# Both halves of the last expert pair's down products issued ahead of the products that carry tokens back, and the carrying matrix transposed between the two up products

## What is computed

```
def run_block(args):
    tok, w, e = args
    xb = x_pad[tok]
    hid = jax.nn.silu(xb @ w1[e]) * (xb @ w3[e])
    return (hid @ w2[e]) * w[:, None].astype(xb.dtype)
...
out = jnp.zeros((T + 1, D), xt.dtype).at[buf_tok].add(y.reshape(P, D))
x = x + hier_moe(rms_norm(x, norm_moe[l]), ...)
```

## Time and profile before

| what | value |
|---|---|
| median of 3 runs | 2251.21 us (2250.78 to 2253.61) |
| span of the profiled execution | 2254.1 us |
| PE busy | 2129.7 us (94%) |
| DVE busy | 743.1 us (33%) |
| ACT busy | 390.4 us (17%) |
| mean DMA rate | 235 GB/s |
| chain that ended last | PE 78%, DMA 13%, DVE 6% |

### The profile page before, as it was taken

How to read it: one execution, slowest core, us unless ns; L and a number is a source line. 1 busy time by engine, 2 the same in 40 slices (tenths; PEclk the granted TensorE clock), 3 DMA queues, 4 the chain that set the end, 5 groups by cost and what they waited for, 6 DMA issues and landing times.

```text
span 2254.1 us, 27568 instructions
## 1 busy us (share of the span) xinstructions
PE 2129.7 (94%) x11793; PEld 1133.6 (50%) x11793; DVE 743.1 (33%) x1754; ACT 390.4 (17%) x745; POOL 242.9 (11%) x250
## 2 busy tenths in 40 slices
PE   8999899999998999889999999999999999999987
PEld 4454566654443433335555567864574533333322
DVE  4125776333001011131277854422232411111104
ACT  3100132121000100011133353220022200000101
POOL 5000312000000000000001141301010000000001
PEclk9999899999999999999998999999999999999989
DMA  8113113158999999996110021124352599999998
GB/s 309 40 38 112 38 38 139 69 236 361 424 422 428 428 418 427 427 399 192 29 30 2 2 77 39 42 108 149 112 213 105 216 420 427 427 428 427 428 425 334
DMA packets 96670, 528.81 MB, mean 235 GB/s; under 512 B 10270, under 2 KB 26323, under 8 KB 69146
## 3 DMA queue, kind: packets, MB, share of 16 engines
q1 hardware_dynamic: 82304, 492.08, 53.8%
q0 software_dynamic: 8160, 17.88, 2.1%
q10 hardware_dynamic: 6074, 16.97, 2.0%
HBM read 509.04 MB, written 30.41 MB: 239 GB/s over the span
## 4 chain that ended last, share of the span: by engine, by line
PE 78%; DMA 13%; DVE 6%; ACT 1%; issue 1%; SPq 1%; ACTq 0%; DVEq 0%
PE ps L204 74%; DMA RING<-in_w_e_up 4%; DMA SC<-in_w_e_up 2%; DMA RING<-in_w 2%; DMA SC<-in_w 2%; DMA XT<-in_w 2%; DMA EX<-in_w_e_up 1%; DMA RING<-in_w_ckv 1%; PE ps L1719 1%; SPq L1633 1%; ACT SC L1876 1%; PE ps L1767 1%; PE ps L2699 0%; PE ps L3294 0%; PE ps L374 0%
## 5 line engine op out<-in xcount | busy, mean ns | idle before, releaser
L204 PE MATMUL ps<-SC 64*64 64x64 f32 (+5 forms) x5408 | 749.4, 349 | 46.7 <-ACT SC L1876 11.1
L204 PE MATMUL ps<-RING,SC 128*64 128x512 f32 (+2 forms) x1648 | 559.1, 587 | 21.6 <-ACT SC L1876 6.2
L204 PEld LDWEIGHTS ps<-SC 64*64 64x64 f32 (+2 forms) x5408 | 333.9, 146 | 345.8 <-issue 292.9
L204 PEld LDWEIGHTS ps<-RING,SC 128*64 128x64 f32 (+2 forms) x1648 | 192.9, 151 | 255.9 <-issue 244.3
L204 PE MATMUL ps<-XT,RING 128*128 128x256 f32 (+2 forms) x944 | 317.6, 489 | 2.4 <-DVE XT L200 1.1
L1944 DVE SCALAR_TENSOR_TENSOR SC<-ps,ST,SC 128x512 f32<-128x512 f32 x30 | 22.5, 751 | 647.7 <-PE ps L204 647.7
L204 PEld LDWEIGHTS ps<-XT,RING 128*128 128x128 f32 (+1 forms) x944 | 176.6, 191 | 116.5 <-issue 99.9
L204 PE MATMUL ps<-RING,XT 128*128 128x512 f32 (+1 forms) x384 | 147.9, 546 | 0.0
L204 PE MATMUL ps<-SC,RING 128*128 128x512 f32 (+2 forms) x504 | 134.6, 432 | 2.3 <-DVE SC L1218 0.8
L204 PE MATMUL ps<-XT,SC 128*64 128x512 f32 (+2 forms) x312 | 120.1, 538 | 4.0 <-DMA SC<-in_w_e_up 3.3
L204 PEld LDWEIGHTS ps<-RING,XT 128*128 128x128 f32 x384 | 69.6, 196 | 76.5 <-issue 75.8
(11 more groups left out here) (485 smaller groups left out, 1956.3 us busy)
## 6 DMA issues: line engine op xcount, KB each, us to landing
SC<-in_w SPq DMA_DIRECT2D x48, 2048.0 KB, 29.5
RING<-in_w SPq DMA_DIRECT2D x36, 2048.0 KB, 33.9
RING<-in_w_in SPq DMA_DIRECT2D x16, 2048.0 KB, 16.2
SC<-in_w_e_gate SPq DMA_DIRECT2D x14, 2048.0 KB, 40.3
SC<-in_w_e_up SPq DMA_DIRECT2D x13, 2048.0 KB, 36.6
SC<-in_w_e_down SPq DMA_DIRECT2D x13, 2048.0 KB, 36.3
RING<-in_w_e_gate SPq DMA_DIRECT2D x11, 2048.0 KB, 33.7
RING<-in_w_e_up SPq DMA_DIRECT2D x11, 2048.0 KB, 40.5
```

What stands on the lines that cost most here:

```text
L204: return e.matmul(out, l, r, start=st, stop=sp, skip_group_check=True)
```

## The change

A new function `hot_p` holds the four transposes of `hot`. It is called within `up_p`, after the last pair's up 0, where the transposes stood after both up products before. In `down_p`, `add_p(e, 0)` and `add_p(e, 1)` are called after both down products of the last pair, where each was called after its own half. What each call issues is the same; the program's other engines are not edited. Both `moe0` and `moe1` are built with it.

```
+        def hot_p(e):
+            b, free = c.take("hot")
+            W.wait_ge(*free)
+            W.wait_ge(*c.on("hot"))
+            for tt in range(NT):
+                i = e.transpose(b[:, tt * 128:(tt + 1) * 128], hot[:, tt * 128:(tt + 1) * 128], ident[:, :])
+            i.then_inc(*c.up("p", "hot T"))
...
         def up_p(e, f, q, banks, w):
...
                 if picked and j == 0:
                     idx_p(e)
+                if f is c and q == LAST and j == 0:
+                    hot_p(e)
...
         def down_p(e, f, q, banks, w):
...
                 i.then_inc(*f.up("p", "down", q, hf))
                 if hf:
                     f.also("p", "w", q, 2)
-                if f is c and q == LAST:
+            if f is c and q == LAST:
+                for hf in range(2):
                     add_p(e, hf)
...
         def p(e):
...
-                if q == LAST:
-                    b, free = c.take("hot")
-                    W.wait_ge(*free)
-                    W.wait_ge(*c.on("hot"))
-                    for tt in range(NT):
-                        i = e.transpose(b[:, tt * 128:(tt + 1) * 128], hot[:, tt * 128:(tt + 1) * 128], ident[:, :])
-                    i.then_inc(*c.up("p", "hot T"))
                 down_p(e, c, q, c.take, w)
```

## The result

Twenty runs of each kernel: before 2253.94 us median (2248.53 to 2259.47), changed 2258.32 us (2254.96 to 2264.83); ratio 1.0023, 95% interval 1.0015 to 1.0031, so 5.2 us slower (3.4 to 7.0); the two medians lie 4.4 us apart. The forecast was +4.1 us, put at 2255.3 us (2252.5 to 2258.2) and called no change as the likeliest. The measured median lies 0.12 us above the range, and the change is a slowdown clear of noise.

A forecast was written before the change was run, and what follows sets the result against it. DVE's 14.4 us of work, starting when the first carrying product is done, was taken to bound the end. +3.67 us (second block) and +0.44 (first) gave +4.1 on the 2251.2 median: 2255.3 us, range 2252.5 to 2258.2.

The forecast's parts named there:

- wait of down 1 for its weights' second part: Last pair: down 1 waits for the down weights' second part, taken as 1.15 us in the second block, bounds 0 to 3.6.
- first add later, second block: DVE's first add after the second block's first carrying product comes at 2234.85, 3.97 us later than before.
- of that DVE makes good, second block: DVE's later adds no longer wait for PE, which returns 0.16 + 0.07 + 0.07 = 0.3 us.
- last add later, second block: DVE's last add ends 3.67 us later, and this goes to the kernel's end in full.
- first add later, first block: DVE's first add in the first block's last pair comes at 1001.85, 4.08 us later than 997.77.
- key products later (bank of tile 2, half 1): After the first block's experts, key products wait for a bank held by DVE's add: 1014.7 instead of 1014.26, 0.44 us.
- transposes' move: Four transposes of `hot`, 0.65 us, are hidden by up 1's wait for weights: taken as 0, bounds 0.65 either way.
- The 1.46 us taken from PE's idle time: PE loses two waits for ACT's copies of down 0 and down 1, 0.76 + 0.70 us of idle a block.
- every case but two: Cases were forecast +4.1, rivals 2253.7, 2258.7, 2257.6 us, all slower; PE's line decides, 2249.7, faster; something else, either sign.
- The norm: After the first block's experts: no bound, its ACT part ending by 1024.2 at worst, PE's transposes coming at 1025.1.
- The rival of the clock: PE's clock falls to the lower level behind down 1's new wait: 2257.6 us, in both blocks 2259.9; chance 0.05.
- the gap that I had read as a pure wait for a transfer: PE's gap of 2.54 us ahead of the first block's key products, until `in_w_ckv` landed at 1014.26.

The follow-up runs named there:

- b2: Changed kernel with down 1 multiplying the first part of the weights again, so without its wait for the second part; ratio to the kernel before 1.0006.
- a3: Kernel before with only the four transposes of `hot` moved between the up products, both blocks; ratio 0.9994.
- b1: Changed kernel with DVE taking tile 0's table rows ahead of its three first adds, both blocks; ratio to the kernel before 0.9995.
- c1: Kernel before with eight unread identity products added on PE behind the first block's last carrying product; ratio 1.0014.
- b3: Changed kernel with eight unread identity products added on PE behind the first block's last carrying product; ratio to the kernel before 1.0025.
- a1: The change made in the second block's expert stage only, the first as in the kernel before; ratio 1.0013.
- d2: Kernel before with only the carrying product of tile 3, half 0, held back until down 1 was issued; ratio 0.9997.

## Why the prediction was wrong

**The mechanism was right, and nearly every term of the sum.**

| step | forecast | measured |
|---|---|---|
| wait of down 1 for its weights' second part | 1.15 us (second block), 1.25 (first) | 1.09 and 1.21; 1.3 when removed (b2) |
| first add later, second block | 3.97 | 3.91 |
| of that DVE makes good, second block | 0.30 | 0.20 |
| last add later, second block | 3.67 | 3.71 |
| first add later, first block | 4.08 | 4.04 |
| key products later (bank of tile 2, half 1) | 0.44 | 0.60 |
| transposes' move | 0 | 0 (a3, -0.2 +- 0.65) |
| sum | 4.1 | 4.3 locally; 4.4 +- 0.4 at equal clock |

The 1.46 us taken from PE's idle time bought nothing, since DVE's 14.4 us start with the first carrying product, and that one was put 3.9 us later. The 0.30 us came to 0.20 because I had counted the whole wait of 0.16 us ahead of an add as won, while 0.10 us lies between two such operations where nothing is waited for (2236.49 + 5.31 = 2241.80 to 2241.90). The error of 0.10 and that of 0.06 in the first add nearly cancel, which is luck. b1 showed the limit from the other side: with the same products on PE, DVE's order alone took 2.45 us off.

**The step that failed** is the one after the sum: "I add the difference to the median: 2251.2 + 4.1 = 2255.3 us." That median stood on three runs of a kernel whose twenty scatter over 11 us with their median at 2253.94, 2.7 us higher. 2253.9 + 4.1 is 2258.0, within 0.3 us of the result. Those three were the first of the twenty, and all of them lie under that median. The profiled execution's span, 2254.1, already disagreed with the base that I took, and I called 0.1% small, though it was two thirds of the effect. Like for like it was more: each run's time on record is 1.7 to 1.9 us longer than its span. The range had no term for the base, so it missed by 0.12 us.

**The second failed step** is the resolution: I let "about 0.2% (4.5 us)" decide between change and no change. A forecast of 0.18% was then called no change, while twenty runs of each narrowed the ratio to +- 0.0008 and put the change outside zero. With every case but two slower than before, the statement should have been: slower, by a size near that bound.

**The norm** was no limit, as forecast: the transposes followed the key products at once in each trace. **The rival of the clock** was put in the wrong place. At down 1's wait nothing fell (24 records in 10.57 us). It was the key products that ran partly at the lower level, behind the gap that I had read as a pure wait for a transfer. That transfer had landed 23.3 us after its issue at 990.45, at 1013.8, half a us ahead of the products, and in c1 the gap stayed without it. The price of 1.7 us there is real, but four of the six traces with the old order in the first block pay it too, the unedited kernel in one of its two, and the mean clocks leave 0.3 +- 0.5 us for the change. The small rest between 4.4 and the ratio's 5.2 is inside the latter's interval.

**How far the sum is confirmed.** The lags in both blocks are those of the forecast in every trace of the changed kernel. That they add up to the total so closely, 4.3 and 4.4, is better than the other versions bear out: at equal clock b1, b2, b3 and a1 are 1.9, 1.5, 2.8 and 1.4 us under the sums of their own lags, and c1 is 1.3 over. In b3 2.6 us more delay of the key products added nothing to the changed kernel's total that can be seen (4.1 against 4.4 us at equal clock). So it stays open how much of the first block's 0.6 us reaches the end.

## What to carry to other kernels

Where one engine feeds another that then works without a gap, ask when the first piece is handed over, not how dense the feeder's line is: here the work and the wait moved ahead of the first piece, 3.9 us, came out 3.7 us later at the end, and filling the feeder's gaps behind it, 0.7 us in d2, brought at most 0.2. Before an operand's use is moved forward, look for its landing, even if nothing waits for it in the trace. For a change of a few us, take lags within the stage, and put the scatter of the baseline into the range when it stands on three runs.

## What the runs showed of the hardware that was not expected

- The place of a stretch at half clock differs between executions of one program: the key products took 10.60 us in one trace of the kernel before and 12.29 us in another. The Trainium skill (TensorE: Matmul & The Clock Gate, "What's actually happening") says that the activity monitor runs free of the program, so that one kernel's slow products vary from run to run; these two traces agree.
- Products put into PE's gap at the end of the expert stage did not fill it: the next stage began 2.65 (c1) and 4.46 us (b3) after them, with its weights landed in c1 3.8 us before. A packet of the instruction queue moved with the gap.
- Totals of twelve runs follow the local lags only to within 1 to 3 us: at equal clock b3 is 2.8 and b1 1.9 us under its local sum, c1 1.3 us over its own 1.9, each +- 0.65. What lies between the two expert stages and differs from kernel to kernel there stays open.
